# Where the second layer's modulation is computed: from the first expert tile to the first scan, and a ring of eight row slots in both layers

## The reference, cut to what matters

```python
mod   = (silu(c)     @ w_mod[i] + b_mod[i]).reshape(B, 6, 1024)   # shift, scale, gate, twice
mod_c = (silu(c_ctx) @ w_mod[i] + b_mod[i]).reshape(6, 1024)
h = _rms(x, norm1) * (1 + sc1) + sh1
p = h @ w_in                                     # gated DeltaNet | FNet | conv module
# gated DeltaNet, per chunk of 64 tokens and head, both directions:
v_new = u_i - w_i @ s
o_i   = q_i @ s + qk_i @ v_new
s     = s * exp(gl_i) + k_i.T @ v_new
x = x + gt1 * (concat(...) @ w_out)
h2 = _rms(x, norm2) * (1 + sc2) + sh2            # then 128 experts per token
act = gelu(u_tab[eid] . h2);  x = x + gt2 * sum_k gw * act * v_tab[eid]
```

## Time and profile before

| | us |
|---|---|
| median of three runs | 5037.53 |
| profiled execution | 5042.18, its span 5040.0 |
| layer 0, `begin` to `gdn_tiles` | 0 to about 631 |
| layer 0, `gdn_scan` | 631.97 (first group) to 698.70 (next phase's first command) |
| layer 0, `peer`, first to last dot product | 881.56 to 2949.07 |
| layer 1, `peer`, first to last dot product | 3692.39 to 5007.19 |
| TensorE, VectorE, ScalarE, GpSimd busy | 80%, 66%, 15%, 33% of the span |
| GpSimd's DMA queue (gathers) | 1342.26 MB, 65.1% of 16 engines' span |

### The profile page before, as it was taken

How to read it: one execution, slowest core, us unless ns; L and a number is a source line. 1 busy time by engine, 2 the same in 40 slices (tenths; PEclk the granted TensorE clock), 3 DMA queues, 4 the chain that set the end, 5 groups by cost and what they waited for, 6 DMA issues and landing times. The chain is left out here.

```text
span 5040.0 us, 53850 instructions
## 1 busy us (share of the span) xinstructions
PE 4048.4 (80%) x19200; PEld 2036.1 (40%) x19200; DVE 3335.9 (66%) x7207; ACT 733.2 (15%) x2486; POOL 1669.2 (33%) x1487
## 2 busy tenths in 40 slices
PE   5997867787788887887887769888768888788776
PEld 2545844333343342433432224477424334343222
DVE  2823456677688787887886646235668878788665
ACT  1112220101111111111110011223111111111001
POOL 0002420334344444444443310044034444444432
PEclk7988989999999999999999989888889999999998
DMA  6110031999999999999999962000489999999998
GB/s 234 46 61 32 3 139 72 421 418 409 399 387 412 417 391 409 410 390 419 387 419 422 418 241 55 21 3 2 155 330 411 412 421 396 421 421 394 421 421 333
DMA packets 256908, 1508.58 MB, mean 299 GB/s; under 512 B 26528, under 2 KB 64800, under 8 KB 83968
## 3 DMA queue, kind: packets, MB, share of 16 engines
q0 software_dynamic: 184320, 1342.26, 65.1%
q1 hardware_dynamic: 72320, 162.88, 8.7%
HBM read 1492.36 MB, written 12.68 MB: 299 GB/s over the span
## 5 line engine op out<-in xcount | busy, mean ns | idle before, releaser
L1827 PE MATMUL ps<-peeb,pediag 128*128 128x512 f32 x5120 | 2497.6, 624 | 658.4 <-DVE pediag L1718 643.0
L1694 POOL DMA_INDIRECT peeb<-in_experts_dram,eid x1280 | 1432.7, 1119 | 2264.9 <-PE ps L1827 1899.4
L1708 DVE CUSTOM_DVE_ANT_0 pedot<-peeb,hc 128x1024 f32<-128x1024 f32 x1280 | 1563.8, 1222 | 426.9 <-DMA peeb<-in_experts_dram,eid 424.7
L1827 PEld LDWEIGHTS ps<-peeb,pediag 128*128 128x128 f32 x5120 | 906.5, 194 | 2154.0 <-DVE pediag L1718 1423.1
L1718 DVE TENSOR_SCALAR pediag<-cst,pege,gw 128x128 f32<-128x128 f32 x1280 | 497.5, 389 | 356.2 <-ACT pege L1791 344.4
L1791 ACT ACTIVATE pege<-peact 128x1 f32<-128x1 f32 x1280 | 259.1, 202 | 2684.8 <-DVE peact L1708 2684.4
L1318 PEld LDWEIGHTS ps<-pehT,arena 128*128 128x128 f32 x2048 | 248.8, 192 | 61.5 <-issue 61.5
L365 PE MATMUL ps<-hT,pjw 128*128 128x512 f32 x576 | 258.1, 603 | 15.5 <-DMA pjw<-in_w_in_dram 15.5
L1318 PE MATMUL ps<-pehT,arena 128*128 128x128 f32 x2048 | 249.3, 275 | 0.0
L1007 POOL TENSOR_TENSOR hT<-cst,gate 128x512 f32<-128x512 f32 x12 | 12.6, 1052 | 633.5 <-SPq L772 632.7
L365 PEld LDWEIGHTS ps<-hT,pjw 128*128 128x128 f32 x576 | 109.5, 193 | 150.9 <-issue 133.5
(11 more groups left out here) (287 smaller groups left out, 3314.6 us busy)
## 6 DMA issues: line engine op xcount, KB each, us to landing
arena<-in_w_mod_dram SPq DMA_DIRECT2D x24, 1024.0 KB, 13.4
pemw<-in_w_mod_dram SPq DMA_DIRECT2D x24, 1024.0 KB, 9.3
peeb<-in_experts_dram,eid POOLq DMA_INDIRECT x1280, 10.7
pjw<-in_w_in_dram SPq DMA_DIRECT2D x36, 512.0 KB, 3.8
arena<-in_peer_wq_dram SPq DMA_DIRECT2D x4, 4096.0 KB, 24.4
pexr<-x_rows SPq DMA_DIRECT2D x18, 512.0 KB, 8.1
w_out<-in_w_out_dram SPq DMA_DIRECT2D x2, 4096.0 KB, 14.3
x_rows<-zs SPq DMA_DIRECT2D x10, 512.0 KB, 2.6
```

The costliest lines, as they stand in the source:

```text
L1694: nc.gpsimd.indirect_dma_start(eb[:, g % RING, :], None, table, bass.IndirectOffsetOnAxis(eid[:, j % 2, k:k + 1], 0)).then_inc(e_in[g % RI ...
L1708: nc.vector.tensor_tensor_reduce(out=dot_out[:], in0=eb[:, g % RING, 0:D], in1=hc[:, j % 2, :], scale=1.0, scalar=0.0, op0=ALU.mult, op1=A ...
L1827: last = nc.tensor.matmul(ps[:, half, :], diag[:, g % DIAGS, :], eb[:, g % RING, D + half * 512:D + (half + 1) * 512], start=k == 0, stop= ...
```

## The change

Layer 1's modulation is no longer computed in `peer` but in `gdn_scan` of layer 0. The scan's SP program loads the 24 pieces into a ring of four buffers (MRING): a part of `hT` that is free in this phase, `hc`, and two new tiles. TensorE works two pieces per step, one after L1120 and one after L1133, into banks 6 and 7. VectorE adds the bias rows after steps 5, 9 and 11, SP stores them, and the phase ends only when they have landed. In `peer` all of this is gone, and RING is 8 in both layers. Cut to its core:

```diff
-def gdn_scan(nc, kit, L, first, qkvT, kt, us, wT, qkd, decs, dts, o):
+def gdn_scan(nc, kit, L, first, hT, qkvT, kt, us, wT, qkd, decs, dts, o):
+    nxt = L + 1 if L + 1 < DEPTH else None
+    MODS = MOD_ROUNDS * KD if nxt else 0
+    MRING = 4
+    ADD_AT = [5, 9, NCH - 1]
...
+        more = sb("mw", [P, 2, MOD_COLS]) if nxt else None
+        free = hT[:, 0:H, :].rearrange("p a b -> p (a b)")
+        pieces = [free[:, 0:MOD_COLS], kit.hc[:].rearrange("p a n -> p (a n)")]
+        pieces += [more[:, k, :] for k in range(2)] if nxt else []
+        row = free[:, MOD_COLS:MOD_COLS + 2 * MOD_N].rearrange("p (a n) -> p a n", a=2)
...
+            @block.sync
+            def _(sp):
+                def biases(r):
+                    if r >= 2:
+                        sp.wait_ge(mod_stored, 16 * MOD_GROUPS * (r - 1))
+                    for j in range(MOD_GROUPS):
+                        for s in range(2):
+                            sp.dma_start(row[32 * j + s:32 * j + s + 1, r % 2, :], mod_bias(kit, nxt, r, j)
+                                         ).then_inc(mod_bias_in[r % 2], 16)
+                def store(r):
+                    sp.wait_ge(mod_rows, MOD_GROUPS * (r + 1))
+                    for j in range(MOD_GROUPS):
+                        sp.dma_start(mod_store(kit, nxt, r, j), row[32 * j:32 * j + 2, r % 2, :]
+                                     ).then_inc(mod_stored, 16)
+                for n in range(MODS):
+                    if n >= MRING:
+                        sp.wait_ge(mod_prod, n - MRING + 1)
+                    sp.dma_start(pieces[n % MRING], mod_weights(kit, nxt, n // KD, n % KD)).then_inc(w_in[n % MRING], 16)
+                    if n == MRING - 1:
+                        biases(0)
+                        biases(1)
+                    elif n == 2 * KD - 1:
+                        store(0)
+                        biases(2)
+                for r in range(1, MOD_ROUNDS if nxt else 0):
+                    store(r)
+                if nxt:
+                    sp.wait_ge(mod_stored, 16 * MOD_GROUPS * MOD_ROUNDS)
...
+                def mod_product(n):
+                    r, k = divmod(n, KD)
+                    if k == 0 and r >= 2:
+                        pe.wait_ge(mod_rows, MOD_GROUPS * (r - 1))
+                    pe.wait_ge(w_in[n % MRING], 16 * (n // MRING + 1))
+                    mod_products(nc, kit, 6 + r % 2, pieces[n % MRING], k).then_inc(mod_prod, 1)
...
                         last.then_inc(vo_ready, 1)
+                    if 2 * s < MODS:
+                        mod_product(2 * s)
                     pe.wait_ge(tail_ready, s + 1)
                     pe.wait_ge(vnew_ready, s + 1)
...
                         last.then_inc(os_ready, 1)
+                    if 2 * s < MODS:
+                        mod_product(2 * s + 1)
...
                             whole_output(nc.vector, c).then_inc(whole, 1)
+                    if nxt and s in ADD_AT:
+                        mod_add(ADD_AT.index(s))
...
-    RING = 6 if nxt else 8
+    RING = 8
...
-                    if i == 0:
-                        for r in range(MOD_ROUNDS if nxt else 0):
-                            modulation(r)
-                            if r >= 1:
-                                modulation_store(r - 1)
-                        if nxt:
-                            modulation_store(MOD_ROUNDS - 1)
-                if nxt:
-                    sp.wait_ge(mod_stored, 16 * MOD_GROUPS * MOD_ROUNDS)
...
-                        if i == 0 and mod_done(k) >= 0:
-                            mod_add(mod_done(k))
...
-                        if j == 2 and nxt:
-                            pe.wait_ge(mod_rows, MOD_GROUPS * MOD_ROUNDS)
...
-                        if i == 0 and mod_at(k) >= 0:
-                            mod_product(mod_at(k))
...
-                    gdn_scan(nc, kit, L, first, qkvT, kt, us, wT, qkd, decs, dts, o)
+                    gdn_scan(nc, kit, L, first, hT, qkvT, kt, us, wT, qkd, decs, dts, o)
```

More of the change, by code:

```diff
@@ L1081, in gdn_scan @@
     with ExitStack() as mem, phase(nc, kit, "zeroed", "v_ready", "s_ready", "vo_ready", "vnew_ready", "os_ready",
-                                   "state_ready", "tail_ready", "decayed", "o_ready", "whole", "whole2", "dve_step") as (
+                                   "state_ready", "tail_ready", "decayed", "o_ready", "whole", "whole2", "dve_step", "mod_prod", "mod_rows",
+                                   "mod_stored", "mod_bias0", "mod_bias1", *["w%d" % k for k in range(MRING)]) as (
             zeroed, v_ready, s_ready, vo_ready, vnew_ready, os_ready, state_ready, tail_ready, decayed, o_ready,
-            whole, whole2, dve_step):
+            whole, whole2, dve_step, mod_prod, mod_rows, mod_stored, mod_bias0, mod_bias1, *w_in):
+        mod_bias_in = [mod_bias0, mod_bias1]
         sb = lambda n, s: mem.enter_context(nc.sbuf_tensor(f"sc{n}_{L}", s, FP32))
@@ L1139, in _, with mod_add @@
                 link = linker(dve, dve_step)
+                def mod_add(r):
+                    dve.wait_ge(mod_bias_in[r % 2], 32 * MOD_GROUPS * (r // 2 + 1))
+                    dve.wait_ge(mod_prod, KD * (r + 1))
+                    for j in range(MOD_GROUPS):
+                        sums = row[32 * j:32 * j + 2, r % 2, :]
+                        nc.vector.tensor_tensor(sums, sums, ps[32 * j:32 * j + 2, 6 + r % 2, :], ALU.add
+                                                ).then_inc(mod_rows, 1)
                 nc.vector.memset(S[:], 0.0).then_inc(zeroed, 1)
@@ L1575, in peer @@
     N = len(tiles)
-    nxt = L + 1 if L + 1 < DEPTH else None
-    RING = 6 if nxt else 8
+    RING = 8
     DIAGS = 3
@@ L1599, in peer @@
         (dotted, gelu_ready, diag_ready, summed, keys_in, row_in, mod_in, xc_in, gate_in, y_gated, x_ready, x_saved,
-         dve_step, mw0, mw1, mod_used, mod_rows, mod_bias0, mod_bias1, mod_stored) = sems[RING:RING + 20]
-        mw_in, mod_bias_in = [mw0, mw1], [mod_bias0, mod_bias1]
+         dve_step) = sems[RING:RING + 13]
         sb = lambda n, s, t=FP32: mem.enter_context(nc.sbuf_tensor(f"pe{n}_{L}", s, t))
@@ L1615, in peer @@
                 "fi": sb("fi", [P, PH, TOPK], U32)[:], "place": sb("place", [P, SLOTS], U32)[:]}
[L1616 to L1620, removed]
-        mod_done = lambda k: mod_at(k - 2) // KD if mod_at(k - 2) >= 0 and mod_at(k - 2) % KD == KD - 1 else -1
+        sc = Scoring(nc, kit, L, 1, sems[RING + 13:], dve_step, bufs)
         ps = kit.ps
@@ L1759, in piece @@
                         sc.expert_number(j)
-                def mod_add(r):
-                    dve.wait_ge(mod_bias_in[r % 2], 32 * MOD_GROUPS * (r // 2 + 1))
-                    dve.wait_ge(mod_used, KD * (r + 1))
-                    for j in range(MOD_GROUPS):
-                        part = row[32 * j:32 * j + 2, r % 2, :]
-                        nc.vector.tensor_tensor(part, part, ps[32 * j:32 * j + 2, 2 + r % 2, :], ALU.add
-                                                ).then_inc(mod_rows, 1)
                 for i in range(N + 1):
```

27 lines of the change are left out of this document (1 added, 26 removed).

## The result

The changed kernel takes 4971.56 us (median of four runs, 4968.85 to 4973.91) against 5039.11 (5037.47 to 5040.97) for the one before: 67.6 us less, a ratio of 0.9866 with a 95% interval of 0.9849 to 0.9883. The forecast was 4976.1 in a range of 4958 to 5008, so both the side and the range were right, and the gain came out 6 us larger than forecast. The two profiled executions, 5042.18 and 4969.22, stand 73.0 apart.

The account below looks back on a forecast made before the run. It took DMA gathers plus full-buffer stalls to bound the expert tiles, and the TensorE-VectorE handoff the scan. Savings of 81.6 us less 20.2 for the scan gave 61.4, so 4976.1 us, range 4958 to 5008.

Parts of the forecast that it names:

- Part 1: Layer 0's first expert tile, rid of the modulation work, falls from 389.24 to 330.86: 58.4 us saved (52.8 to 59.8).
- Part 2: Layer 0's ring, six to eight: saves 5.7 us in tile 1, 17.2 in tiles 2 to 4, 0.3 in tile 5.
- Part 3: Modulation work moved into layer 0's scan lengthens it by 20.2 us (14 to 36).
- The plain step: Scan step with two products on TensorE in line grows from 4.55 to 6.2 us.
- The first step: Scan's first step, at the low clock and waiting for piece 0, goes from about 7 to 9.1 us.
- The additions: VectorE's bias-add rounds in the scan show 0.6 us after step 5 and 2.5 after step 9.
- SP: Scan's SP queue of pieces, biases and stores delays nothing: 0 us, up to 10 in the range.
- The end: From the scan's last step to the next phase, 8.93 becomes 12.7 us: +3.8 for last adds and stores.
- A: Rival: the deeper ring gives nothing in layer 0's expert tiles; time 5004.9 us, chance 0.12.
- B: Rival: TensorE's clock stays low through the scan, +78 us; time 5034, chance 0.05.
- C: Rival: slow landing of weight pieces makes the kernel slower; at 25 us each, time 5052; chance 0.03.
- The case for a much better result: Products in the scan better hidden than thought; time near 4968 us, chance 0.05.

Follow-up runs that it names:

- a1: Changed kernel with layer 0's ring of row slots left at six instead of eight (the move only); 5003.62 us, ratio 0.9926.
- a0: The changed kernel run again, unedited, as yardstick for the others; 4972.44 us, ratio 0.987.
- b2: Changed kernel with every product in the scan worked twice, the first copy into an unused bank; 4983.45 us in one run.
- x2: Changed kernel with seven row slots in layer 0 instead of eight; 4983.43 us, ratio 0.9892.
- a2: Changed kernel with nine row slots in both layers and three score buffers instead of four; 4966.73 us, ratio 0.9857.
- b1: Changed kernel with VectorE's six placing operations spread over slots 66 to 91; 4958.63 us, ratio 0.9842.
- b4: Changed kernel with two weight-piece buffers in the scan instead of four (MRING); 4984.11 us in one run.
- a3: Changed kernel with the scan's additions put where VectorE waits, a row buffer and bank per round, and stores' landing awaited later; 4966.22 us, ratio 0.9858.
- after: The changed kernel itself, as first measured and profiled against the kernel before; 4971.56 us, ratio 0.9866.

## Why the prediction was right, point by point

**The bound was read rightly.** The expert tiles are set by the gathers' transfers and the stalls above them, the scan by TensorE and VectorE. Both showed: the tiles shrank by the pieces taken out and by the ring, the scan lengthened by TensorE's time.

**Part 1** (58.4) measured 56.7. The reading that layer 0's first tile becomes layer 1's first tile held within 1.7 us. Its lower bound did not: with six slots this tile is 339.88, not the 336.48 that I took from its neighbours, so the move alone gives 49.4 there, the ring the other 7.4, and the bound of 52.8 was too high. A tile that begins a stage isn't its neighbours' mean.

**Part 2** (23.2 in all) measured 31.6. The step that failed in size is the second tile, 5.7 against 12.7. I had named a cause and chosen the low side of it: a deeper ring may hide the stall at the fetch of the latents' modulation. a1 splits the 12.7: with six slots the tile is 343.03, so 3.1 came with the move alone (one profile of each kernel), to which I had given nothing here, and 9.6 with the ring. Of these, 4.0 to 5.7 stand in the tile's first 32 slots, where the third tile gains 0.1 to 1.8, and the rest at its end as in every tile. The stall is not gone: with eight slots the first 32 still take 87.9 to 89.5 us. That it is the fetch is read from its place; no run takes the fetch away. The three middle tiles, 17.2, gave 18.7 between the profiled pair and 14.9 between a1 and a0 on one chip, so 17.2 was about right. But the reason with which I supported it, two buffers are 5.0 us more of transfer during one stall, is only half borne out: rows do land ahead during a stall, but the worth falls from slot to slot (22.2, 11.6, 2.5 us over five tiles) and is not one transfer's time a slot, so the agreement of 5.0 with 5.7 was chance.

**Part 3** (20.2) measured 20.5, by errors that cancel.
- *The plain step*, 6.2 foreseen, 5.95 measured: 0.25 too much in each of ten steps, 2.5 us. The 0.09 by which a product began late between two expert matmuls isn't there in the scan. The first product begins 1.90 us into the step, just before L1169's record ends, where I had it at 1.98 + 0.09; from L1184 to the next L1160 it is 1.02 + 0.97, where I had 1.05 + 1.06. The Trainium skill (TensorEngine Tiling (Array Packing), Key Properties) says that changing the tiling mode drains the engine. b2 doesn't speak against it: the first of two products costs 0.11 us more than the second. The 0.97 already holds this, so I counted a price of the change once too often.
- *The first step*, 9.1 foreseen, 8.79 measured. The product's weight load waited 0.43 us for the piece, and the product began where L1169 ended, so the wait cost TensorE next to nothing.
- *The additions*, 0.6 and 2.5 foreseen, 0.8 and 4.3 measured (6.73 and 10.22 less 5.95). The first is right. Of the second, 2.64 us is the wait that I foresaw and 1.6 the low clock behind it: a1, with the same code and the same wait of 2.64 us, has the clock at 1.00 there and a step of 8.67 against 10.22.
- *SP*, 0 foreseen with up to 10 in the range, 1.6 measured. I had named this place, piece 16 behind the stores and biases, and set it at 0 with 15 us against 15 us: it was a tie and came out 1.3 to 1.6 late in three runs (this one, a0, x2) and on time in three others (a1, a2, b1). The bias commands cost 0.29 to 0.31 us each (16 in 4.96, 8 in 2.29), not 0.52; it is the wait for the stores that decides, 4.6 to 4.8 us in the three late runs and 1.3 to 1.6 in the three others.
- *The end*, +3.8 foreseen, +3.35 measured.

So the sum's 61.4 became 67.7 in its own terms (88.3 - 20.5, rounded). The second tile alone is 7.0 of these 6.3 us, and the other terms cancel to -0.7. Layer 1's tiles and the earlier start of the scan, which no edit explains, gave the profiled pair another 4.6; 0.7 of its 73.0 stand elsewhere.

**The rivals.** A fell by a1. B, the clock staying low, didn't happen: 1.00 from 640 to 700 here and in every run with the products but that with two piece buffers (b4, 0.94); TensorE's low clock cost 1.6 us in one step. C's mechanism exists (b4 shows it) but needs a ring half as deep to be seen at all. The range held, though its upper end, 5008, left out my own worst sum, 5020.7. The case for a much better result, products better hidden than I thought, was right about the plain step, but for another reason, since nothing hides them: they only cost 0.97 instead of 1.06.

**What stays open:** why the stores of round 0 land after 1.3 to 1.6 us in some runs and 4.6 to 4.8 in others with the same commands ahead of them; and what keeps a scoring tile 6 to 10 us above the quiet one once the ring has eight slots.

## What to carry to other kernels

Look for a stage whose DMA is idle before shortening one that is bound by it: 24 pieces of 1 MB, moved from a stage at 416 GB/s to one at 2 GB/s, cost nothing as transfers (57.8 us for eleven steps with and without them). What they cost there is the products, the additions and the places where these and SP's commands stand. When work is put into a chain that two engines hand back and forth, cost it by the engine that becomes the bound (here TensorE's own 5.95 us), and put the second engine's share where that engine waits anyway: in a3 the place of twelve small additions, of the waits in SP's queue, of one product and of the last wait was worth 8 of the 20 us. A deeper ring's worth has to be measured slot by slot, as it falls off quickly, and a bound for one tile is to be taken from a tile with the same loads.

## What the runs showed of the hardware

- A wait of about 2.6 us on TensorE was followed by the low clock in some runs and not in others. In after, a0 and x2, where a wait of 1.3 to 1.6 us for a piece lay two steps ahead of it, the clock fell (0.58 in after); so it did in b4, where 4.11 us lay two steps ahead (the wait 2.54, L1184 then 1.97). In a1, a2 and b1 without that wait it stayed (1.00 in a1). That is four against three and no proof of the cause. The two groups of a1 after its wait, and the window that holds them:

```profile
702.89 1.16 PE L1178 MATMUL ps<-scvn,sctail 64*128 64x128 f32 x16 [2.64 <-DVE scvn L1207]
703.98 1.09 PE L1184 MATMUL ps<-scvn,qkd 64*64 64x128 f32 x16
```

```profile
702.80:705.90 3.10, 3.01 (x40) 1.96 (x40) 2.25 (x3) 0.00 (x0) 0.41 (x1) 1.00 0.10 36
```

- Transfers at 420 GB/s left the scan's engines where they were (57.8 us for eleven steps, with them and without).
- A product between groups of other shapes costs 0.97 us in line, one right behind another product 0.86 (b2). The 0.11 us between them is the most that a change of shape showed here, if it is that.
- Small DMA commands on SP follow each other at 0.3 us (8 in 2.29), while the same queue's wait for four stored rows takes 1.3 to 4.8 us.
- A deeper ring shows at a tile's end: the last 32 of 128 slots take 78.4 to 80.5 us with six slots and 73.5 to 76.1 with eight, and a ninth slot is worth no more than the spread of the runs.
